# A last MLP whose down projection goes by tokens, in seven block products instead of eight

## The chip, the cores and the metric

The kernel runs on one core of a Trainium2 chip. The metric is the device time of one execution in microseconds. A run of the profiler gives, beside it, every instruction's start and duration on TensorE (PE for products, PEld for loading weights into it), VectorE (DVE), ScalarE (ACT), GpSimd (POOL) and the queue engine SyncE (SP), and the DMA transfers.

## The reference, cut to what matters

The program is a network of two blocks on one sequence of 512 tokens with 1,024 channels. The first has attention, pooling and a state space mixer, then a mixture of experts. The second has two layers: latent attention and an MLP, then an S5 mixer and an MLP. The change is in the last MLP and the last norm, which both layers of the second block compute like this:

```python
def sq_relu_mlp(h, w1, b1, w2, b2):
    a = jax.nn.relu(h @ w1 + b1)
    return (a * a) @ w2 + b2

    shift, scale, gate = modulation(cs, mod_ffn_w[i], mod_ffn_b[i])
    h = x * (1.0 + scale) + shift
    y = sq_relu_mlp(h, mlp_w1[i], mlp_b1[i], mlp_w2[i], mlp_b2[i])
    x = layer_norm_2(ALPHA * x + (1.0 + gate) * y, ln_ffn_g[i], ln_ffn_b[i])
```

Here w1 is 1,024 x 4,096 and w2 is 4,096 x 1,024, both float32; the norm is over the channels of each token.

## The kernel before

Every stage is a block in which each engine has its own instruction list, and semaphores order them; a stage ends when all engines have reached its end. A float32 matrix is split in two float32r parts, `high` (a copy, ScalarE, line 3797) and `low` (matrix minus high part, VectorE, line 3912), and a product is the sum of three: high x high, low x high, high x low (function `three`, line 3722). One product is 128x128 loaded by 512 columns.

`tail_stage` (line 3601) is called twice, for layer 0 (with S5 parameters and the S5 input beside it) and for layer 1 (`last`). It walks over units `n`. A unit is one load of 1,024 KB of weights into one of four buffers `w_second` (line 3679), its high and low part into one of two buffers `late_parts`, and 2 x 8 x 3 = 48 products. Units 0 to 3 are the mixer's output projection, then come the first norm (`mix_norm`) and two steps, each of 8 up units (w1) and 8 down units (w2). All results have channels on partitions and tokens along the row: weights are loaded into TensorE, activations move. The order is written out by hand:

- TensorE starts unit `n` when its low part is done (line 3736).
- ScalarE may write the high part of unit `n + 2` when the products of unit `n` are done (line 3796), since the two buffers alternate. VectorE then makes the low part.
- SP loads unit `n` when the low part of unit `n - 4` is done (line 3678).
- After an up unit ScalarE takes relu out of the banks (line 3820), VectorE squares (3945), ScalarE and VectorE split the square into `hidden` (3826, 3951). During the first step ScalarE also scales the residual `x` (3810).
- After every second down unit VectorE adds gate times the bank to `x` (3927). In the last step it also prepares sums for the norm (3547, 3556, 3564).

The last norm (`TokenNorm`, line 3484) needs sums over partitions, for which TensorE multiplies by a matrix of ones (3504 to 3518). Then come variance and root on rows of 512 tokens (3531 to 3538), centring and scaling of eight channel tiles (3585, 3598), gain and offset (3891), and since the output has tokens on rows, 32 transposes (3788), copies (3830) and eight stores (3695). Small matrices before the norm's end keep TensorE at work (`fill`, line 158).

GpSimd (line 3698) forms a few vectors at a stage's start and has nothing else to do in these stages. In layer 0 of `tail_stage`, VectorE computes S5 parameters between the units (`beside`) into one buffer `room`, which SP stores part by part (line 4077) and VectorE writes again for the next part (line 4310).

## Time and profile before

| | us |
|---|---|
| median of three runs | 2656.68 |
| the three runs | 2660.67, 2656.08, 2656.68 |
| span of the profiled execution | 2654.8 |
| busy TensorE products / weight loads | 2503.1 / 1989.2 |
| busy VectorE / ScalarE / GpSimd | 1729.9 / 1139.0 / 63.4 |
| last MLP stage, first product to end of span | 2221.1 to 2654.8 |
| of it units 4 to 35 | 2281.4 to 2632.2 |

The span is the time from the first to the last instruction of one profiled execution. That execution's time with what lies around the span isn't given apart; the median of the runs is 1.9 us above the span. Busy times of different engines overlap. DMA over the whole: 427.44 MB.

### The profile page before, as it was taken

How to read it: one execution, taken by the hardware profiler on the slowest of the kernel's cores; microseconds unless marked ns; L12 is line 12 of the kernel's file. 1: busy time of each engine (PE TensorE's matmuls, PEld its weight loads, DVE VectorE, ACT ScalarE, POOL GpSimd, SP SyncE). 2: the span in 40 equal slices, each digit the busy share in tenths (PEclk: the TensorE clock that was granted, in tenths of full speed). 3: DMA queues.
4: the chain of work that ended last, by engine and by line, in shares of the span. 5: the costliest groups of instructions: out<-in, count | busy, mean ns of one | idle time of the engine just before them, and what ended most of it. 6: DMA issues, size and time to landing. Idle time of an engine off the chain costs nothing. (4 is left out here: it accounts for less than half of the span.)

```text
span 2654.8 us, 33834 instructions
## 1 busy us (share of the span) xinstructions
PE 2503.1 (94%) x13321; PEld 1989.2 (75%) x13321; DVE 1729.9 (65%) x2508; ACT 1139.0 (43%) x1641; POOL 63.4 (2%) x166
## 2 busy tenths in 40 slices
PE   7999899999989999899988899999999989999998
PEld 5666578777767877788875457888888877788886
DVE  4899545588875666899965565677766664632435
ACT  5444422255564235688853344522324253531323
POOL 0000000000000001000001000000000000000000
PEclk9999999999999988999999999999999899999999
DMA  7887727333235734999962203234332423233321
GB/s 263 264 284 270 245 82 276 91 104 95 80 104 191 257 61 167 355 420 419 417 250 92 78 27 104 80 119 135 111 111 77 127 87 121 65 107 98 95 80 32
DMA packets 299502, 427.44 MB, mean 161 GB/s; under 512 B 27690, under 2 KB 213533, under 8 KB 289488
## 3 DMA queue, kind: packets, MB, share of 16 engines
q1 hardware_dynamic: 289424, 395.13, 43.4%
q0 software_dynamic: 5392, 20.97, 2.0%
q10 hardware_dynamic: 4528, 9.18, 0.9%
q8 instruction: 106, 1.74, 0.3%
q14 instruction: 52, 0.43, 0.0%
HBM read 384.11 MB, written 41.14 MB: 160 GB/s over the span
## 5 line engine op out<-in xcount | busy, mean ns | idle before, releaser
L3724 PE MATMUL banks<-big,late_parts 128*128 128x512 f32 x1920 | 443.0, 393 | 5.9 <-PEq L151 3.8
L3724 PEld LDWEIGHTS banks<-big,late_parts 128*128 128x128 f32 x1920 | 363.3, 189 | 84.1 <-issue 6.1
L3724 PE MATMUL banks<-h_parts_second,late_parts 128*128 128x512 f32 x1440 | 331.1, 390 | 4.7 <-DVE h_parts_second L3936 4.7
L3724 PEld LDWEIGHTS banks<-h_parts_second,late_parts 128*128 128x128 f32 x1440 | 271.0, 188 | 61.2 <-issue 5.1
L3912 DVE TENSOR_TENSOR late_parts<-w_second,late_parts 128x2048 fp32r<-128x2048 f32 x69 | 158.1, 2292 | 218.7 <-ACT late_parts L3797 218.5
L2379 DVE TENSOR_TENSOR expert_parts<-w,expert_parts 128x2048 fp32r<-128x2048 f32 x102 | 232.7, 2288 | 21.7 <-ACT expert_parts L2375 20.8
L3797 ACT ACTIVATE late_parts<-w_second 128x2048 fp32r<-128x2048 f32 x69 | 132.0, 1914 | 255.9 <-PE banks L3724 255.9
L1344 PE MATMUL banks<-h_parts,ssm_parts 128*128 128x512 f32 x960 | 229.0, 396 | 0.8 <-DVE ssm_parts L1611 0.4
L2375 ACT ACTIVATE expert_parts<-w 128x2048 fp32r<-128x2048 f32 x102 | 194.8, 1916 | 60.6 <-PE banks L2386 54.7
L1344 PEld LDWEIGHTS banks<-h_parts,ssm_parts 128*128 128x128 f32 x960 | 178.5, 188 | 43.3 <-issue 6.4
L2386 PE MATMUL banks<-expert_parts,expert_xt 128*128 128x512 f32 x816 | 192.4, 395 | 4.0 <-DVE expert_xt L2367 4.0
L2386 PEld LDWEIGHTS banks<-expert_parts,expert_xt 128*128 128x128 f32 x816 | 153.6, 190 | 36.5 <-DVE expert_xt L2367 4.6
L881 PE MATMUL banks<-h_parts,front_parts 128*128 128x512 f32 x552 | 137.6, 399 | 0.0
L551 PE MATMUL banks<-h_parts,front_parts 128*128 128x512 f32 x576 | 132.3, 391 | 2.7 <-PEq L151 2.7
L551 PEld LDWEIGHTS banks<-h_parts,front_parts 128*128 128x128 f32 x576 | 108.0, 188 | 26.4 <-issue 4.2
L3820 ACT ACTIVATE tail_r<-banks,cols 128x512 f32<-128x512 f32 x64 | 40.5, 685 | 198.5 <-PE banks L3724 198.5
L551 PE MATMUL banks<-h_parts,ssm_parts 128*128 128x512 f32 x480 | 111.5, 394 | 5.9 <-DVE h_parts L1965 3.1
L881 PEld LDWEIGHTS banks<-h_parts,front_parts 128*128 128x128 f32 x552 | 101.5, 190 | 19.7
L3945 DVE TENSOR_TENSOR tail_q<-tail_r 128x512 f32<-128x512 f32 x64 | 41.4, 689 | 111.5 <-ACT tail_r L3820 111.4
L1134 DVE SCALAR_TENSOR_TENSOR attention_mod_sum<-w,silu_c,attention_mod_sum 128x512 f32<-128x512 f32 x147 | 110.4, 751 | 4.8 <-DMA w<-in_mod_ffn_w_dram 0.3
L551 PEld LDWEIGHTS banks<-h_parts,ssm_parts 128*128 128x128 f32 x480 | 91.0, 190 | 26.1 <-issue 3.9
L2386 PE MATMUL banks<-expert_parts,expert_ht 128*128 128x512 f32 x408 | 98.9, 399 | 3.0 <-ACT experts_y L2879 3.0
(703 smaller groups left out, 3851.2 us busy)
## 6 DMA issues: line engine op xcount, KB each, us to landing
w_second<-in_mlp_w_dram SPq DMA_DIRECT2D x64, 1024.0 KB, 5.2
w<-in_w_exp_gate_dram SPq DMA_DIRECT2D x34, 1024.0 KB, 9.6
w<-in_w_exp_up_dram SPq DMA_DIRECT2D x34, 1024.0 KB, 9.4
w<-in_w_exp_down_dram SPq DMA_DIRECT2D x34, 1024.0 KB, 9.2
w<-in_w_in_dram SPq DMA_DIRECT2D x64, 512.0 KB, 4.6
w<-in_mod_mix_w_dram SPq DMA_DIRECT2D x24, 1024.0 KB, 5.1
w<-in_mod_ffn_w_dram SPq DMA_DIRECT2D x23, 1024.0 KB, 5.9
w<-in_w_in_dram SPq DMA_DIRECT2D x16, 1024.0 KB, 5.7
```

The costliest lines, as they stand in the source:

```text
L551: mm = pe.matmul(out, self.parts[:, n % 2, w, kk, f * P:(f + 1) * P], x[:, v, kk, :], start=(start and kk == 0 and j == 0), stop=(stop and ...
L881: mm = pe.matmul(ps[:, bank, :], parts[:, j, w, kk, :], k.hp[:, x, kk, :], start=(kk == 0 and n == 0), stop=(kk == KD - 1 and n == 2))
L1134: ins = dve.scalar_tensor_tensor(out=acc, in0=w, scalar=by, in1=acc, op0=ALU.mult, op1=ALU.add)
L1344: mm = pe.matmul(ps[:, t % 2, :], parts[:, t % SPLITS, w, kk, :], k.hp[:, x, kk, :], start=(kk == 0 and j == 0), stop=(kk == KD - 1 and j ...
L2375: act.activation(self.high_part(h), self.raw(h), ACT.Copy).then_inc(self.high_done, 1)
L2379: dve.tensor_tensor(self.low_part(h), self.raw(h), self.high_part(h).bitcast(F32), ALU.subtract).then_inc(self.low_done, 1)
L2386: mm = pe.matmul(out, x[:, v, first + kk, :], self.tile(h, w, kk), start=(start and kk == 0 and j == 0), stop=(stop and kk == KE - 1 and j ...
L3724: mm = pe.matmul(ps[:, bank(n, f), :], w_part(n, w)[:, kk, f * P:(f + 1) * P], x[:, v, kk, :], start=(first_chunk(n) and kk == 0 and j == ...
L3797: act.activation(w_part(n, 0), raw_half(k, n), ACT.Copy).then_inc(s["high_done"], 1)
L3820: act.activation(r[:, c % 2, :], ps[:, bank(n, c % HT), :], ACT.Relu, bias=k.cols[:, b1 + at:b1 + at + 1]).then_inc(s["relu_done"], 1)
L3912: dve.tensor_tensor(w_part(n, 1), raw_half(k, n), w_part(n, 0).bitcast(F32), ALU.subtract).then_inc(s["low_done"], 1)
L3945: dve.tensor_tensor(q[:, c % 2, :], r[:, c % 2, :], r[:, c % 2, :], ALU.mult).then_inc(s["squared"], 1)
```

## The change

The stage for the last layer becomes a function of its own, `closing_stage`; `tail_stage` keeps layer 0 alone, with one addition, `later.form(pool)`.

- **Seven products.** Each step of the down projection takes a quarter of the hidden channels (1,024). The hidden matrix is seen as 2 x 2 blocks (even and odd tiles of 128 channels by the two halves of the tokens), and the weights as 2 x 2 blocks (even and odd tiles of rows by the two halves of the output channels). Of these, VectorE forms four sums of hidden blocks, and there are seven block products of 24 products each instead of eight; the outputs are sums of these products (the scheme of Strassen and Winograd). Hidden blocks are loaded into TensorE and weights move, so results have tokens on partitions.
- **Four steps** of 4 up units and 7 down units instead of two of 8 and 8: 48 units instead of 36. One up unit of the next step stands ahead of each block of down units, except the last block.
- **Sums of weight blocks.** Four of the seven products need sums of weight blocks. They are formed in DRAM by GpSimd's DMAs during layer 0's MLP: eight transfers of 4 MB, four of which add to their destination.
- **Sums of products.** Two of the seven products (FOUR, 21) stay in their banks over all steps, the other five are added to tiles on chip (`add`) after each unit, and joined in the last step (`join`, `take`).
- **Residual.** `x` is turned to tokens on partitions by 32 transposes after the up units (1,1), (1,2), (1,3) and (2,0), through banks 4 and 5, and copied back by ScalarE.
- **Last norm per token.** GpSimd multiplies sums by the gate (read as a row through DRAM) and adds `x`; VectorE takes mean and variance of each token's row; two token tiles are normed by ScalarE and GpSimd, two by VectorE; four stores of 512 KB.

The core of the diff:

```diff
+class WeightSums:
...
+    def form(self, pool):
...
+        pool.dma_start(two, self.block(0, 0)).then_inc(s["sum_two"], 16)
+        pool.dma_start(right, self.block(0, 1)).then_inc(s["sum_right"], 16)
+        pool.wait_ge(s["sum_two"], 16)
+        pool.dma_start(two, self.block(0, 1), accum_op=ALU.add).then_inc(s["sum_two"], 16)
+        pool.wait_ge(s["sum_right"], 16)
+        pool.dma_start(right, self.block(1, 1), accum_op=ALU.add).then_inc(s["sum_right"], 16)
+        pool.wait_ge(s["sum_two"], 32)
+        pool.dma_start(three, two).then_inc(s["sum_three"], 16)
+        pool.wait_ge(s["sum_three"], 16)
+        pool.dma_start(three, self.block(1, 1), accum_op=ALU.add).then_inc(s["sum_three"], 16)
+        pool.wait_ge(s["sum_three"], 32)
+        pool.dma_start(four, three).then_inc(s["sum_four"], 16)
+        pool.wait_ge(s["sum_four"], 16)
+        pool.dma_start(four, self.block(1, 0), accum_op=ALU.add).then_inc(s["sum_four"], 16)
+        pool.wait_ge(s["sum_right"], 32)
+        pool.wait_ge(s["sum_four"], 32)
...
+PRODUCT_11, PRODUCT_THREE, PRODUCT_RIGHT, PRODUCT_FOUR, PRODUCT_TWO, PRODUCT_22, PRODUCT_21 = range(7)
...
+def closing_stage(k, layer, w_mix, x_parts, big, divided, sums, out):
...
+    BANK = {PRODUCT_11: 4, PRODUCT_THREE: 6, PRODUCT_RIGHT: 4, PRODUCT_FOUR: 2, PRODUCT_TWO: 6, PRODUCT_22: 4, PRODUCT_21: 0}
...
+            sp.dma_start(k.gate_row.rearrange("o (c p) -> p (o c)", p=P), k.mod[:, gate_ffn:gate_ffn + KD], allow_slow_non_contiguous=True).then_inc(s["gate_stored"], 16)
+            for n in range(4, N):
+                if n == N - 2:
+                    sp.wait_ge(s["gate_stored"], 16)
+                    sp.wait_ge(s["tile_done"], tiles_to(N - DOWN - 1))
+                    sp.dma_start(gate, k.gate_row.to_broadcast([P, D])).then_inc(s["gate_loaded"], 16)
+                    for dst, src in ((gain, k.ins["ln_ffn_g_2"][layer:layer + 1]), (shift, k.ins["ln_ffn_b_2"][layer:layer + 1])):
+                        sp.dma_start(dst, src.to_broadcast([P, D])).then_inc(s["rows_loaded"], 16)
+                sp.wait_ge(s["low_done"], n - 3)
+                sp.dma_start(raw(n), source(n)).then_inc(k.raw_loaded[n % 4], 16)
...
+            for first, half, after in ((2, 0, 2), (2, 1, 4), (0, 0, 8), (0, 1, 8)):
+                pool.wait_ge(s["joined"], after)
+                pool.wait_ge(s["w_joined"], 2)
+                for t in (first, first + 1):
+                    pool.tensor_tensor(z(t, half), z(t, half), gate[:, half * STRIP:(half + 1) * STRIP], ALU.mult).then_inc(s["v_step"], 1)
+                    n += 1
+                for j, t in enumerate((first, first + 1)):
+                    pool.wait_ge(s["v_step"], n - 1 + j)
+                    row = z(t, half).rearrange("p (c n) -> p c n", n=P)
+                    pool.tensor_tensor(row, row, x_tile(t, half), ALU.add).then_inc(s["v_ready"], 1)
...
+            def room(i, q, j):
+                if q == PRODUCT_11:
+                    if i > 0:
+                        pe.wait_ge(s["z_step"], reads(i - 1, PRODUCT_22, j))
+                    if i == 1:
+                        pe.wait_ge(s["x_copied"], 2 * TB)
...
+                    for kt in range(4):
+                        pe.wait_ge(s["hidden_low"], UP * i + kt + 1)
+                        for j in range(2):
+                            mm = down_three(n, i, q, j, kt)
...
+            def combine(g):
+                dve.wait_ge(s["relu_done"], HT * (g + 1))
...
+                dve.tensor_tensor(flat, r[:], r[:], ALU.mult).then_inc(s["squared"], 1)
+                dve.wait_ge(s["squared"], g + 1)
+                n = comb.start(dve.tensor_tensor(e[:, LEFT], e[:, FIRST], e[:, SECOND], ALU.subtract))
+                comb.start(dve.tensor_tensor(e[:, SIDE], e[:, BEFORE], e[:, FIRST], ALU.subtract))
+                comb.after(n)
+                comb(dve.tensor_tensor(e[:, ALL], e[:, LEFT], e[:, BEFORE], ALU.subtract))
+                dve.tensor_tensor(e[:, ACROSS], e[:, ALL], e[:, BEHIND], ALU.add).then_inc(s["combined"], 1)
...
+            def take(n, p):
...
+                for j in range(2):
+                    dve.wait_ge(s["tile_done"], HT * n + j + 1)
+                    end(dve.tensor_tensor(tmp(p, j), ps[:, BANK[p] + j, :], gate[:, half * STRIP:(half + 1) * STRIP], ALU.mult))
+                    for first, ready in places:
+                        t = first + j
+                        dve.wait_ge(s["v_ready"], ready + j)
+                        end(dve.tensor_tensor(z(t, half), z(t, half), tmp(p, j), ALU.add))
+                        if (p, first) != (PRODUCT_TWO, 2):
+                            end.start(dve.bn_stats(stats[:, t, half, :], z(t, half)))
...
+            for n in range(RES, N):
+                if up(n):
+                    i, m = up(n)
+                    combine(UP * i + m)
+                    if EXTRA + 1 < n + 2 < N:
+                        low(n + 2)
+                    if i == 0 or m > 0:
+                        hidden_low(UP * i + m)
+                else:
+                    i, p = down(n)
+                    if p in (PRODUCT_11, PRODUCT_THREE, PRODUCT_RIGHT) or (i < STEPS - 1 and p not in KEPT):
+                        add(n)
+                        if i == STEPS - 1:
+                            join(p)
+                    elif i == STEPS - 1:
+                        dve.wait_ge(s["gate_loaded"], 16)
+                        take(n, p)
+                    if n + 2 < N:
+                        low(n + 2)
...
-    tail_stage(k, 1, k.ins["ssm_w_out_2"][0], low_half, big, parts, out=out)
+    closing_stage(k, 1, k.ins["ssm_w_out_2"][0], low_half, big, parts, sums, out)
```

## Rows read from the trace of the kernel before

**Rows 1.** The page: busy time and share of the engines; weight loads and us to landing.

```profile
PE 2503.1 (94%) x13321; PEld 1989.2 (75%) x13321; DVE 1729.9 (65%) x2508; ACT 1139.0 (43%) x1641; POOL 63.4 (2%) x166
...
w_second<-in_mlp_w_dram SPq DMA_DIRECT2D x64, 1024.0 KB, 5.2
```

**Rows 2.** Chain of waits, last MLP: start us, us, what.

```profile
2281.43 306.34 PE banks L3724 x1344
...
2588.62 43.57 PE banks L3724 x192
```

**Rows 3.** Windows: length, busy by engine, clock, DMA; then S5 input products in time order.

```profile
2281.40:2632.20 350.80, 350.77 (x1539) 290.12 (x1540) 140.16 (x142) 111.07 (x122) 0.00 (x0) 1.00 0.24 78
2632.20:2654.80 22.60, 14.94 (x80) 9.75 (x79) 11.82 (x19) 12.45 (x20) 0.00 (x0) 0.89 0.31 93
...
2045.52 22.95 PE L4761 MATMUL banks<-big,h_parts_second 128*128 128x512 f32 x96
```

**Rows 4.** Last 10 us in order of time (start, length), and the stores' landing.

```profile
2648.07 0.42 PEld L3788 LDWEIGHTS banks<-ident,x 128*128 128x128 f32 x4 [0.77 <-ACT x L3891]
2648.07 0.66 PE L3788 MATMUL banks<-ident,x 128*128 128x128 f32 x4 [0.53 <-ACT x L3891]
...
out_dram<-big_plain SPq DMA_DIRECT2D x8, 256.0 KB, 2.2
```

**Rows 5.** In order of time: first products after the first norm, first hand-overs.

```profile
2281.43 2.90 PE L3724 MATMUL banks<-h_parts_second,late_parts 128*128 128x512 f32 x6 [2.37 <-DVE h_parts_second L3936]
...
2303.56 1.27 ACT L3820 ACTIVATE tail_r<-banks,cols 128x512 f32<-128x512 f32 x2 [11.51 <-PE banks L3724]
...
2307.56 1.24 ACT L3820 ACTIVATE tail_r<-banks,cols 128x512 f32<-128x512 f32 x2
...
2308.71 1.90 ACT L3797 ACTIVATE late_parts<-w_second 128x2048 fp32r<-128x2048 f32 x1
...
2310.64 2.29 DVE L3912 TENSOR_TENSOR late_parts<-w_second,late_parts 128x2048 fp32r<-128x2048 f32 x1 [1.09 <-ACT late_parts L3797]
```

**Rows 6.** Groups of instructions: busy us, mean ns of one | idle before.

```profile
L3912 DVE TENSOR_TENSOR late_parts<-w_second,late_parts 128x2048 fp32r<-128x2048 f32 x69 | 158.1, 2292 | 218.7 <-ACT late_parts L3797 218.5
L3797 ACT ACTIVATE late_parts<-w_second 128x2048 fp32r<-128x2048 f32 x69 | 132.0, 1914 | 255.9 <-PE banks L3724 255.9
L3945 DVE TENSOR_TENSOR tail_q<-tail_r 128x512 f32<-128x512 f32 x64 | 41.4, 689 | 111.5 <-ACT tail_r L3820 111.4
...
L4312 DVE TENSOR_TENSOR s_room<-s_room,s_tmp 128x256 f32<-128x256 f32 x32 | 13.6, 425 | 1.1
```

**Rows 7.** Lines 1330, 2719, 2721: ns min/median/max.

```profile
L1330 POOL TENSOR_TENSOR ssm_sq<-ssm_sq x12: 1279/1292/2607, 593.2 to 815.5; 128x512 f32<-128x512 f32 x12
...
L2719 DVE TENSOR_TENSOR routing_room<-expert_parts_plain,routing_both_b x3: 1207/1210/1216, 1055.0 to 1061.1; 128x1024 f32<-128x1024 f32 x3
...
L2721 DVE TENSOR_TENSOR expert_parts_plain<-routing_room,routing_both_b x3: 1925/1934/1991, 1056.3 to 1062.4; 128x1024 f32<-128x1024 f32 x3
```

**Rows 8.** GpSimd and S5 buffer in order of time, then transfers: KB, us to landing.

```profile
1765.74 0.37 SPq L4077 DMA_DIRECT2D s_inputs<-s_room  x1
...
1772.31 0.41 DVE L4310 TENSOR_TENSOR s_room<-s_held,s_b 128x256 f32<-128x256 f32 x1
...
2043.01 1.81 POOL L4249 MEMSET late_parts_plain<- 128x2048 f32 x1 [444.71 <-POOLq L151]
...
expert_rows<-pool_zeros POOLq DMA_DIRECT2D x1, 12288.0 KB, 43.8
...
s_inputs<-s_room SPq DMA_DIRECT2D x8, 512.0 KB, 2.7
```

**Rows 9.** Last MLP's start: first product, then windows (the clock stands third from last).

```profile
2221.12 19.09 PE L3724 MATMUL banks<-big,late_parts 128*128 128x512 f32 x72 [3.76 <-PEq L151]
...
2223.00:2225.00 2.00, 2.00 (x6) 1.61 (x5) 0.68 (x1) 2.00 (x3) 0.10 (x1) 0.50 0.87 231
2225.00:2227.00 2.00, 2.00 (x7) 1.53 (x7) 1.62 (x1) 2.00 (x3) 0.00 (x0) 0.64 0.83 292
```

563 lines of the change are left out of this document (460 added, 103 removed).

## The prediction

> **What bounds the kernel now.** I read the page's busy shares and slices first, then the chain of waits, then the closing stage by windows and in order of time. The page's first lines: TensorE is busy 94% of the span, VectorE 65%, ScalarE 43%, GpSimd 2% [rows 1]. In the stretch that the change rewrites the chain is TensorE alone: 306.34 us without a break, a pair of small sums, and 43.57 us for 192 products [rows 2], that is 226.9 ns per 128x512 product. Its granted clock there is 1.00, VectorE is busy 140 of 351 us, ScalarE 111, the DMA engines 24% [rows 3]. After the last product come 22.6 us (2632.2 to 2654.8) in which the sums over tokens, the norm, eight groups of turns and eight stores hand over to each other, VectorE and ScalarE about 12 us each [rows 3]. So the change can gain in two places, in the number of products and in that end, and it loses wherever a hand-over that had 10.9 us of cover (48 products) now has 5.45 us (24).
>
> **Products.** Before, the last down projection is 16 units of 48 products, 768. Afterwards it is 4 steps of 7 block products, each 2 token tiles x 4 hidden tiles x 3 parts = 24: 672. They have the same form (128x128 loaded, 512 columns moving). 96 x 0.2269 = -21.8 us. The pair of sum products in the middle (0.86) goes too: -0.9. Bounds: below, the same 226.9; above, the S5 input products, 96 in 22.95 us, 239 ns each [rows 3]. These load strided weights, which the new ones don't, so I take 226.9; at 239 the 672 would cost 8 us more.
>
> **Turns.** 32 transposes leave the end and go between up units. Four take 0.42 us of weight loading, 0.66 from the first start to the last end [rows 4]. I take 0.11 each and 0.1 per pair of groups: +3.8 us, bounds 3.4 and 5.3.
>
> **Hand-overs in the up units.** One up unit asks of ScalarE two relus (0.68 each), the high part of a weight tile (1.92), and the high part of seven sums of 256 (1792 columns, by 1.92 for 2048: 1.68); of VectorE a square of 1024 (1.21), four additions of 256 (0.42 each, one overlapped), the weight tile's low part (2.29) and 1792 columns of low part (2.02) [rows 5 to 7]. From the second relu (0.75 after the unit's end) combining ends at 3.6, the next low part at 5.9. That fits under 10.9 us, with three exceptions.
> - First pair. Before, the relus of unit 4 start at 2303.56, those of unit 5 at 2307.56, and unit 7's low part ends at 2312.93, 2.6 us ahead of need (unit 5 ends at 2304.6, unit 6 10.9 later) [rows 5]. Now combining takes 2.8 instead of two overlapped squares (1.3), and the second relu waits behind the longer high part and two residuals: second relu ends at 2312.1, combining at 2315.0, low part at 2317.3: +1.8 us.
> - Up to down. A down unit covers only 5.45 us of the 5.9: +0.45 each time, twice (the third is hidden by the next point).
> - The last turned tiles lie in banks 4 and 5, which the next down product writes. Their copies stand on ScalarE behind relu and a high part: 0.75 + 1.92 + two copies of 0.6 = 3.9 us after the unit, the turns take 0.9: +3.0 us.
>
> **Last change from up to down.** No up unit covers it. The fourth hidden pair needs relu 0.75, combining to 3.6, high part to 5.3, VectorE's weight tile to 5.9 ahead of it, its own low part to 8.0. TensorE has 18 products (4.1 us) of cover: +4.0 us.
>
> **Down units in steady state.** Tile done, high part to 1.95, low part to 4.25, and 5.45 are needed; the additions of product sums (two of 0.68) fit before. Loads: 1,024 KB land in 5.2 us [rows 1]. A load is issued when the low part four units before is done and its high part starts two units before its use, so at 5.45 per unit it has 17 us. I cost the 12 extra loads, 12 high and 12 low parts at nothing: the products hide them with 1.2 us to spare per unit, and what comes on top of that is lost unit by unit. SP also gets a store of 1,024 single values ahead of its first load; that load has 26 us until its high part starts.
>
> **Last step, where VectorE becomes the bound.** Clock from the end of the last up unit (0). With the 4.0 wait, product 11 ends at 9.45, THREE at 14.9, RIGHT at 20.35. After RIGHT VectorE adds (0.7), joins four tiles (2.8) and ends the low part at 26.2, when TensorE wanted it at 25.8: +0.45. After FOUR it multiplies, adds and takes statistics for two tiles; with 0.7 per operation, and GpSimd (1.29 per operation on 512 columns [rows 7]) delivering its first sum at 23.9 + 3 x 1.29 = 27.8, it ends at 31.1, low part 33.4: +1.75. After TWO, six operations and the small aggregations more: low part at 41.7, +2.85. Together 5.05 us, products end at 47.2. Then VectorE still has product 22 (to 45.9), product 21 (to 50.5), four passes of 1024 columns (1.21 [rows 7] and a wait each) to 55.6, and a 512 KB store: 256 KB land in 2.2 [rows 4], 512 KB in 2.7 [rows 8], with its issue 3.1: 58.7. The end shrinks from 22.6 to 11.5: -11.1. No row shows the statistics instruction. A 512-column operation takes 0.69; 256 columns take 0.43 [rows 6] and 1024 take 1.21 [rows 7]; eight of them stand in this chain, so -2 to +4 us around 0.7.
>
> **Clock.** After 3.76 us of idle the granted clock read 0.50 (1.2 GHz) for the next 4 us and 0.64 for two more [rows 9], some 2.7 us lost; after 2.37 us of idle six products took 2.90 [rows 5], where six at 226.9 take 1.36. The waits of 3.0, 4.0 and 2.85 are of this kind. All lost: 8; none: 0; I take +4, since part of the last is hidden behind VectorE.
>
> **The sums of weight blocks** are formed in the MLP before: GpSimd issues eight transfers of 4,096 KB, DRAM to DRAM, four of them adding, six in a row of dependence. GpSimd is idle for 444.7 us there, until 2043.0 [rows 8]. The stage can't end before the last wait there. Its only large transfer now, 12,288 KB, took 43.8 us [rows 8]: 14.6 us for 4,096. Eight at that price, all one after another: 117 us. No row shows an adding transfer; it may cost up to (444.7 - 4 x 14.6) / 4 = 97 us each before it counts. The Trainium skill (Collectives: The Full Stack, "The bandwidth ceiling") says a reducing transfer runs at half the rate of a copy because it reads two sources; by that, as an estimate, 29 us each and 175 us in all, and no run here shows it yet. Beside weight loads, which come 39 us before need and land in 5.2, doubling costs nothing. The tightest user is the S5 buffer: its store lands in 2.7 us, and VectorE writes the buffer again 6.6 us after the issue [rows 8]. I take 0; bounds 0 and rival B.
>
> **Sum.** -21.8 - 0.9 + 3.8 + 1.8 + 0.9 + 3.0 + 4.0 + 5.05 - 11.1 + 4 = -11.25. The profiled execution's span is 2654.8, its own whole time isn't given apart; the median of the three runs, 2656.68, is 1.9 above the span, and I carry that over: **2645.4 us**.
>
> **Rivals.**
> - B, the adding transfers don't fit (slower). For: a transfer that reads, adds and writes 2 KB rows in strict turn has 128 rows per engine (2,048 over 16), and at the 2.2 us of the shortest landing [rows 4] per row it takes 282 us, four take 1,126, 740 us too long: about 3385 us. Against: nothing asks for strict turn, and plain transfers don't behave so. It decides from 97 us per adding transfer; at 100 the gain is gone. Chance 0.09.
> - C, GpSimd is late in the last step. It has sixteen operations there, and all of them read on-chip memory beside VectorE. Its operation took 2.61 once in twelve against 1.29, and a VectorE addition beside its row scatter took 1.93 where the same shape takes 1.21 [rows 7]. At 2.6 each the queue is 16 operations from 12.2: its last four sums come at 40.8, 43.4, 51.2 and 53.8 instead of 27.8 to 34.3; VectorE's low part for 21 moves from 41.7 to 57.6, +15.9: 2661 us, no gain. Chance 0.08. The Trainium skill (SBUF — State Buffer, "Who interferes with whom") states that a VectorE instruction with two inputs there contends with a GpSimd one that reads; by that rule this is what would happen, while by the median of the rows it isn't.
> - D, the hand-overs cost more than I sum, half clock after each wait (+4) and statistics at 1.2 (+4), and the turns at their bound (+1.5): 2655, no measurable change. Chance 0.11.
> - E, the middle waits vanish, since copies and residuals find gaps: the 3.0, 1.8 and the clock's 4 go: 2637. Chance 0.10.
> - Forecast: 0.62.
>
> **Range and chances.** About 0.2% (5.3 us) can be told from no change. Of the forecast's 0.62 nearly all is faster; with E and a little of C and D: faster 0.73. Same: most of D, half of C: 0.14. Slower: B and the rest: 0.13. B is left out of the range, its far end can't be held: 2635 to 2659.
>
> **What would show it.** 672 down and 768 up products at 227 ns each. TensorE idle: one wait near 4 us ahead of the last block, one near 3 us behind the last turns, two or three in the last 30 us that end on VectorE's low part. Less than 12 us from the last product to the end. GpSimd's last wait of the stage before well ahead of 2043, and that stage as long as now. It is wrong if that stage grows, if down units before the last step wait for weights, or if the end is longer than 16 us.

## The result: slower by 0.9%, where 0.4% faster was forecast

| | median us | runs | ratio to before, 95% interval |
|---|---|---|---|
| before | 2658.39 | 2656.08 to 2660.67 (4) | |
| changed | 2682.34 | 2679.82 to 2689.42 (4) | 1.0093 (1.0076 to 1.0109) |
| forecast | 2645.4 | range 2635 to 2659 | |

The profiled execution of the changed kernel took 2689.42 us, its span is 2687.7 (before: 2654.8). It is the slowest of its four, so I compare stages and not whole spans; each stage is read from one profiled execution. Stages are cut at GpSimd's operations, which stand at the start of each: the MLP of layer 0 from the first operation on `vec` to the fill of `late_parts`; the S5 and GLU stages from there to the next operation on `vec`; the last MLP from there to the end.

| us | MLP of layer 0 | S5 and GLU | last MLP |
|---|---|---|---|
| before | 450.3 | 178.1 | 433.7 |
| changed | 474.0 | 184.2 | 434.0 |
| forecast of the difference | 0 | 0 | -11.25 |
| measured | +23.7 | +6.1 | +0.3 |

So two things went wrong: a loss in a stage that I had costed at nothing, and a gain that didn't come in the stage that was rewritten. The medians of the whole lie 23.95 us apart, which is what the two MLPs give together (23.7 + 0.3).

The +0.3 flatters the change. After the same wait of 3.76 us at the start of the last MLP, the first 96 products took 24.53 us in the kernel before (granted clock 0.73 over the first 10 us) and 23.42 in the changed one (0.85); after the same wait of 2.37 us behind the first norm, the first twelve took 4.25 and 2.84 (0.67 and 1.00 over 4.6 us). No edit touches these; both kinds of start occur among the profiles of kernels that share this code. Start for start, the changed stage is 2.8 us longer. A difference of under 3 us between two last MLPs can be of this kind.

The page of the changed kernel, the lines that answer to [rows 1] (the engine's busy us and share; the weight loads of both MLPs and us to landing):

```profile
PE 2489.4 (93%) x13175; PEld 1975.2 (73%) x13175; DVE 1821.9 (68%) x2578; ACT 1166.0 (43%) x1632; POOL 118.8 (4%) x196
...
w_second<-in_mlp_w_dram SPq DMA_DIRECT2D x60, 1024.0 KB, 5.3
```

TensorE is busy 13.7 us less (2503.1 to 2489.4). Fewer products alone should give 21.8; part of the difference is that products last longer at a lower granted clock (the last three blocks below take 5.9 us more than three times 5.45). VectorE is busy 92 us more. The median landing of a weight tile hides what happened. In the MLP of layer 0, from 1590 to 1700 us, the tiles land so (least, median, most us):

```profile
DMA to landing us min/median/max: 18.0/43.2/54.1
```

ScalarE's operations on them in order of time (start, length; in brackets idle before and what ended it):

```profile
1650.24 1.91 ACT L3828 ACTIVATE late_parts<-w_second 128x2048 fp32r<-128x2048 f32 x1 [13.17 <-DMA w_second<-in_mlp_w_dram]
1663.87 1.91 ACT L3828 ACTIVATE big<-w_second 128x2048 fp32r<-128x2048 f32 x1 [11.72 <-DMA w_second<-in_mlp_w_dram]
```

and TensorE's waits for the norm behind them:

```profile
1658.69 2.07 PE L3510 MATMUL banks<-tail_sums,ones 128*128 128x512 f32 x2 [11.30 <-DVE tail_sums L3557]
1667.87 2.07 PE L3512 MATMUL banks<-tail_sums,ones 128*128 128x512 f32 x2 [7.11 <-DVE tail_sums L3565]
```

In the kernel before the same stretch has 5.2/5.3/8.8 us to landing. This is a chain: the tile is late, ScalarE is stuck on its high part with the squares of the norm queued behind it, VectorE's sums are late, TensorE is idle. ScalarE's two waits make 24.9 us. TensorE waits 19.9 us for the norm's sums (11.30, 7.11 and one more of 1.51), where the kernel before has one wait of 1.29; the stage's other 5 us go with a granted clock of 0.87 instead of 0.98 from 1593 to 1700 us.

In the last MLP TensorE's waits (in brackets), in order of time from the first hand-over:

```profile
2346.53 22.06 PE L4191 MATMUL banks<-h_parts_second,late_parts 128*128 128x512 f32 x96 [0.74 <-DVE late_parts L4394]
2374.42 32.93 PE L4209 MATMUL banks<-late_parts,big 128*128 128x512 f32 x144 [0.40 <-DVE late_parts L4394]
2457.45 39.97 PE L4209 MATMUL banks<-late_parts,big 128*128 128x512 f32 x168 [2.97 <-ACT x L4322]
2546.78 32.94 PE L4209 MATMUL banks<-late_parts,big 128*128 128x512 f32 x144 [0.39 <-DVE late_parts L4394]
2620.13 14.92 PE L4209 MATMUL banks<-late_parts,big 128*128 128x512 f32 x54 [3.69 <-DVE big L4421]
2635.62 5.73 PE L4209 MATMUL banks<-late_parts,big 128*128 128x512 f32 x24 [0.57 <-DVE late_parts L4394]
2644.77 7.39 PE L4209 MATMUL banks<-late_parts,big 128*128 128x512 f32 x24 [3.42 <-DVE late_parts L4394]
2656.38 7.14 PE L4209 MATMUL banks<-late_parts,big 128*128 128x512 f32 x24 [4.22 <-DVE late_parts L4394]
2668.86 7.69 PE L4209 MATMUL banks<-late_parts,big 128*128 128x512 f32 x24 [5.34 <-DVE late_parts L4394]
```

Down to 2620 these are the waits that the prediction named, at its prices or below. Then come 13.6 us in four waits where it had 5.05 in three. Behind the last three of them, a block of 24 products takes 7.1 to 7.7 us instead of 5.45: over its first 4 us the granted clock reads 0.50 to 0.75. In the kernel before it was 1.00 up to the last product and 0.89 over the end behind it [rows 3]; from the last step to the end it is now 0.81:

```profile
2612.20:2687.70 75.50, 47.10 (x169) 36.34 (x167) 63.45 (x60) 19.24 (x22) 42.40 (x20) 0.81 0.21 77
```

(columns as in [rows 3]: VectorE busy 63.45 of 75.50, GpSimd 42.40). From VectorE's operations of that step, in order of time:

```profile
2623.82 1.29 DVE L4440 TENSOR_TENSOR closing_sums<-closing_sums,closing_z_late 128x512 f32<-128x512 f32 x2
2630.36 3.00 DVE L4445 TENSOR_TENSOR closing_z_late<-closing_z_late,closing_sums 128x512 f32<-128x512 f32 x2
2633.28 2.28 DVE L4394 TENSOR_TENSOR late_parts<-w_second,late_parts 128x2048 fp32r<-128x2048 f32 x1
2635.49 1.27 DVE L4432 TENSOR_TENSOR big_plain<-big_plain,banks 128x512 f32<-128x512 f32 x2
2636.79 3.42 DVE L4448 TENSOR_TENSOR big_plain<-big_plain,closing_sums 128x512 f32<-128x512 f32 x2
2648.42 1.68 DVE L4467 TENSOR_TENSOR big_plain<-big_plain,closing_r 128x512 f32<-128x512 f32 x1 [3.11 <-POOL big_plain L4179]
2650.13 0.69 DVE L4469 BATCH_NORM_STATS2 closing_stats<-big_plain 128x6 f32<-128x512 f32 x1
2664.50 4.31 DVE L4394 TENSOR_TENSOR late_parts<-w_second,late_parts 128x2048 fp32r<-128x2048 f32 x1
```

and from GpSimd's:

```profile
2625.34 4.52 POOL L4174 TENSOR_TENSOR closing_z_late<-closing_z_late,h_parts_second_plain 128x512 f32<-128x512 f32 x2 [48.86 <-DVE closing_sums L4440]
2633.44 4.53 POOL L4174 TENSOR_TENSOR closing_z_late<-closing_z_late,h_parts_second_plain 128x512 f32<-128x512 f32 x2 [0.63 <-DVE closing_z_late L4445]
2663.99 2.67 POOL L4185 TENSOR_TENSOR big_plain<-big_plain,h_parts_second_plain 128x1024 f32<-128x1024 f32 x1
```

Two additions of 512 columns take 1.29 alone, 3.00 and 3.42 beside GpSimd. A low part takes 2.28 where it began first (2633.28 against 2633.44) and GpSimd's pair beside it takes 4.53 (2.58 by the 1.29 of [rows 7]); it takes 4.31 where GpSimd was first (2663.99 against 2664.50). Additions that read a product's bank (1.27 for two) and the statistics (0.69) keep their length.

### The profile page after: what moved, and what is told of

It is laid out like the page before. It is cut to its first block and busy times, and to the rows that moved or that the text cites. A ratio compares the mean times of both kernels' runs of the same rounds, so it can differ in the third digit from the quotient of the medians.

```text
span 2687.7 us, 33664 instructions
## 1 busy us (share of the span) xinstructions
PE 2489.4 (93%) x13175; PEld 1975.2 (73%) x13175; DVE 1821.9 (68%) x2578; ACT 1166.0 (43%) x1632; POOL 118.8 (4%) x196
## 5 line engine op out<-in xcount | busy, mean ns | idle before, releaser
L3766 PE MATMUL banks<-big,late_parts 128*128 128x512 f32 x960 | 221.0, 392 | 2.2 <-DVE late_parts L3919 2.2
L1345 PEld LDWEIGHTS banks<-h_parts,ssm_parts 128*128 128x128 f32 x960 | 180.5, 190 | 43.6 <-issue 6.5
L3766 PEld LDWEIGHTS banks<-big,late_parts 128*128 128x128 f32 x960 | 181.3, 189 | 41.0 <-DVE late_parts L3919 2.4
L4209 PE MATMUL banks<-late_parts,big 128*128 128x512 f32 x672 | 164.2, 406 | 21.0 <-DVE late_parts L4394 14.3
L4209 PEld LDWEIGHTS banks<-late_parts,big 128*128 128x128 f32 x672 | 132.0, 198 | 52.5 <-DVE late_parts L4394 16.9
L4394 DVE TENSOR_TENSOR late_parts<-w_second,late_parts 128x2048 fp32r<-128x2048 f32 x46 | 107.7, 2340 | 57.0 <-ACT late_parts L4289 56.9
L3919 DVE TENSOR_TENSOR late_parts<-w_second,late_parts 128x2048 fp32r<-128x2048 f32 x35 | 80.1, 2292 | 93.2 <-ACT late_parts L3828 93.1
L4289 ACT ACTIVATE late_parts<-w_second 128x2048 fp32r<-128x2048 f32 x46 | 88.0, 1913 | 118.3 <-PE banks L4209 105.5
L3828 ACT ACTIVATE late_parts<-w_second 128x2048 fp32r<-128x2048 f32 x35 | 66.9, 1914 | 143.3 <-PE banks L3766 130.1
L552 PEld LDWEIGHTS banks<-h_parts,front_parts 128*128 128x128 f32 x576 | 109.2, 190 | 26.8 <-issue 4.2
```

Source lines behind the costliest of these rows:

```text
L552: mm = pe.matmul(out, self.parts[:, n % 2, w, kk, f * P:(f + 1) * P], x[:, v, kk, :], start=(start and kk == 0 and j == 0), stop=(stop and ...
L1345: mm = pe.matmul(ps[:, t % 2, :], parts[:, t % SPLITS, w, kk, :], k.hp[:, x, kk, :], start=(kk == 0 and j == 0), stop=(kk == KD - 1 and j ...
L3766: mm = pe.matmul(ps[:, bank(n, f), :], w_part(n, w)[:, kk, f * P:(f + 1) * P], x[:, v, kk, :], start=(first_chunk(n) and kk == 0 and j == ...
L3919: dve.tensor_tensor(w_part(n, 1), raw_half(k, n), w_part(n, 0).bitcast(F32), ALU.subtract).then_inc(s["low_done"], 1)
L4209: mm = pe.matmul(ps[:, BANK[q] + j, :], hidden(STATIONARY[q], v)[:, kt, j * P:(j + 1) * P], strip_part(n, w)[:, kt, :], start=(kt == 0 and ...
L4289: act.activation(w_part(n, 0), raw_half(k, n), ACT.Copy).then_inc(s["high_done"], 1)
```

## The experiments

Each line gives the stages as above; the last column is the whole time's ratio to the kernel before, run on the same chip, with its interval.

| kernel | MLP of layer 0 | last MLP | median us | ratio |
|---|---|---|---|---|
| b_form | 476.8 | 433.7 | 2681.07 | 1.0086 (1.0070 to 1.0103) |
| e_late | 503.6 | 434.1 | 2713.38 | 1.0215 (1.0198 to 1.0232) |
| e_s5 | 454.3 | 435.1 | 2662.70 | 1.0020 (1.0009 to 1.0031) |
| e_attn | 449.1 | 434.0 | 2701.10 | 1.0158 (1.0139 to 1.0177) |
| e_swap | 470.0 | 433.8 | 2680.30 | 1.0079 (1.0053 to 1.0105) |
| e_split | 450.4 | 437.1 | 2659.46 | 1.0006 (0.9997 to 1.0016) |
| c_nopool | 478.4 | 422.9 | 2679.62 | 1.0081 (1.0058 to 1.0104) |
| c_fix | 474.1 | 429.7 | 2683.60 | 1.0095 (1.0072 to 1.0118) |
| c_scratch | 476.7 | 438.1 | 2694.26 | 1.0137 (1.0112 to 1.0162) |
| c_all | 477.4 | 430.9 | 2686.45 | 1.0109 (1.0083 to 1.0135) |
| g_turns | 474.4 | 429.5 | 2683.82 | 1.0100 (1.0081 to 1.0119) |
| best | 450.5 | 421.0 | 2648.81 | 0.9967 (0.9955 to 0.9980) |

The kernels with the transfers at the old place or in the attention spread by 5 to 12 us between their own runs, so there a whole time tells less than a stage. The last MLP of kernels that don't touch it took 433.7 to 435.1, but for e_split's 437.1. Of its 3.1 us over the changed kernel, 1.5 lie in the first 96 products (24.91) and 1.6 in the twelve behind the first norm (4.42), the slow start told above. The last step by itself, from the end of the last up unit to the end of the span, is the cleaner number: 75.5 us in the changed kernel, e_late, e_attn, e_swap and e_split (74.0 in e_s5).

The diffs below are excerpts. Those of the last MLP's runs are shortened to what they do, and some lines in them are words and not code.

### Where the 24 us in the MLP of layer 0 come from

**b_form**, one part alone:

```diff
 # kernel before, GpSimd in the MLP of layer 0
             step(pool.tensor_scalar(vec[:, O_SHIFT], sh2, ALPHA_2, None, ALU.mult))
+            later.form(pool)
```

> One part of the change alone: the kernel before, and in the MLP of layer 0 GpSimd also issues the eight transfers that form the sums of weight blocks, right after its column work, as in the changed kernel. Nobody reads the sums. Theory T (the transfers delay the first weight tiles of that MLP, the rest of the change is about even): that MLP goes from 450.3 us to about 474, and the whole time from 2658.4 to 2682 (2678 to 2686), the whole loss of the change. Rival R1 (the loss is a difference of placement, alignment or code between the programs): the MLP stays within 3 us of 450.3 and the whole within 5 us of the kernel before.

476.8 in the stage, 2681.07 in all. The transfers, which nobody reads here, cost the kernel before what the whole change cost. Theory T holds.

**e_late** and **e_s5**, the start of the transfers:

```diff
+            pool.wait_ge(s["low_done"], 12)        # e_late
+            pool.wait_ge(s["dt_loaded"], 32)       # e_s5
+            pool.wait_ge(s["b_loaded"], 64)        # e_s5
             later.form(pool)
```

> The changed kernel with one wait more: GpSimd starts the eight transfers only when the twelfth weight tile of the MLP of layer 0 is divided, when the small S5 loads have long landed and loads run ahead of need. Theory T1 (only the first tiles suffer, because there the loads start with nothing in hand): the MLP is back at 450 to 453, the whole at 2657 to 2662, level with the kernel before. Rival T2 (plain share of the bandwidth: 28 MB more have to pass at any time, and the weight tiles lose as much later): the MLP stays at 465 or more, the whole above 2672.

503.6 and 2713.38. Theory T1 failed, and rival T2's bounds came by another mechanism than it named: it was not the weight tiles. The first waits are gone, a worse one is there. The S5 buffer `s_room` from 1750 to 1900 us: for how many us and times VectorE stood idle for its stores, and the stores' landing:

```profile
  DMA s_inputs<-s_room: 70.8, 7
...
DMA to landing us min/median/max: 9.1/10.4/26.7
```

TensorE's first waits behind it:

```profile
1798.63 14.05 PE L3767 MATMUL banks<-big,late_parts 128*128 128x512 f32 x48 [12.03 <-DVE late_parts L3920]
1816.57 13.65 PE L3767 MATMUL banks<-big,late_parts 128*128 128x512 f32 x48 [3.89 <-DVE late_parts L3920]
1839.72 13.98 PE L3767 MATMUL banks<-big,late_parts 128*128 128x512 f32 x48 [9.49 <-DVE late_parts L3920]
```

The stores of 512 KB land in 10.4 us instead of 2.7 [rows 8], VectorE writes the buffer again after 6.6, stands still, and its next low part, which TensorE needs, is late. The prediction had named this buffer as the tightest user, with both numbers, and then taken 0.

> The changed kernel with another wait: GpSimd starts the eight transfers when the six S5 loads that stand ahead of the weight loads in SyncE's queue (8,192 pieces of 64 bytes the largest) have landed, still before the first up products. Theory T1a (in the changed kernel 709 packets of SyncE's queue carried 0.05 MB in 10 us while 765 of GpSimd's carried 3.13 MB: packet by packet in turn, the small pieces are held up behind the large): most of the loss goes, the MLP falls to 450 to 458 and the whole to 2658 to 2667. Rival T1b (the weight tiles are slow at half a share, 14 us per MB while GpSimd's transfers add, whatever stands ahead): 12 us or more stay, the whole above 2671.

454.3. A start 4.7 us later, behind the small loads, gives back 20 of 24 us: ScalarE has no wait for these tiles any more. Of the 4 us that stay, 3.51 are one wait of TensorE behind VectorE, which stood 14.8 us for the S5 buffer's stores. How the two queues share, in the changed kernel from 1606 to 1616 us, and from 1636 to 1646, while two transfers add (packets, MB, share of the 16 engines; q0 carries GpSimd's transfers, q1 SyncE's):

```profile
q0 software_dynamic: 765, 3.13, 95.5%
q1 hardware_dynamic: 707, 0.05, 4.9%
```

```profile
q0 software_dynamic: 748, 1.53, 82.4%
q1 hardware_dynamic: 742, 0.75, 27.8%
```

Packet for packet the queues get nearly the same number; small packets carry 0.05 MB in the time in which large ones carry 3.13. The Trainium skill (DMA: Bandwidth & Descriptors, "Queues, rings and completion order") says that a DMA engine takes turns between queues packet by packet; the trace agrees: 765 packets against 707, and in e_swap below, from 1630 to 1680 us, 4,419 against 4,416 (11.12 MB and 0.79). The prediction did not weigh it.

**e_swap** tells the order from the share of the bandwidth:

```diff
-            beside.load(sp, s)
             for n in range(4, N):
                 ...
+                if n == 6:
+                    beside.load(sp, s)
```

> The changed kernel with its transfers where they were, and the order in SyncE's queue turned round: the six small S5 loads are issued behind the first three weight tiles of the MLP of layer 0 instead of ahead of them (in the kernel before the values of the first are used near 1682 us). Theory T1a (the weight tiles were late because 8,192 small pieces ahead of them in their queue went one for one with GpSimd's large packets): the first weight tile lands 12 to 20 us after its issue instead of 47, ScalarE's waits for it (13.2 and 11.7) go, the MLP takes 452 to 460 and the whole 2659 to 2668; what remains is the S5 loads' own lateness and the second place, the buffer's stores. Rival T1b (half a share of the bandwidth, whatever stands ahead): the tile still lands after more than 30 us, ScalarE waits 10 us or more, the MLP stays above 468.

The first waits went as T1a says: ScalarE starts the two tiles at 1636.55 and 1638.35 without waiting (1650.24 and 1663.87 in the changed kernel). But the stage fell only to 470.0 and the whole to 2680.30, where at most 460 and 2668 were expected, a miss of 10 and 12 us. The hold-up moved behind the small loads. SyncE's queue in order of time (start and length of the issues):

```profile
1621.99 29.41 SPq L4589 DMA_DIRECT2D s_room<-in_ssm_b_re_dram  x2
1651.44 44.22 SPq L4589 DMA_DIRECT2D s_room<-in_ssm_b_im_dram  x2
1695.70 16.70 SPq L3727 DMA_DIRECT2D w_second<-in_mlp_w_dram  x4
```

and TensorE's wait for the first of those tiles:

```profile
1708.04 24.56 PE L3767 MATMUL banks<-h_parts_second,late_parts 128*128 128x512 f32 x96 [15.09 <-DVE late_parts L3920]
```

The issue of four small loads, 1.9 and 2.7 us for two each in the kernel before, took 73.6: SyncE could not go on, and the next tiles were issued only at 1695.70. Whatever stands behind the small pieces waits; which tile that is depends on the order. Large transfers beside the tiles alone are not the cause: in e_s5 the tiles land in 24.8 us at the median there (35.9 at most), also far from 5.3, and TensorE waits for them no more than 0.56 us.

**e_attn**, another stage for the transfers:

```diff
 # attention of the second block
+        @block.gpsimd
+        def _(pool):
+            later.form(pool)
 # MLP of layer 0
-            later.form(pool)
+            later.ready(pool)       # the last two waits of form
```

> The changed kernel with the eight transfers moved one stage ahead: GpSimd issues them in the attention of the second block, where the kernel before has its DMA engines busy 13 to 24% from 1400 to 1590 us and GpSimd idle for 165 us; only the wait for the last two stays in the MLP of layer 0. Theory T (the transfers cost time only where somebody needs a transfer soon: the small S5 loads with the first weight tiles behind them, and later the S5 buffer's stores): the MLP is at 450 to 452 again, the attention longer by 0 to 4 us (its loads of 192 and 128 KB are issued most of a head ahead), the whole at 2657 to 2662. Rival T3 (any 28 MB of adding transfers disturb whatever runs beside them, by the memory and not by the queue): the attention is longer by 10 us or more, or the MLP stays above 460, and the whole is above 2668.

The MLP is at 449.1, but the whole at 2701.10. The attention waits for its own loads, which land in 9.0 and 11.6 us instead of 2.5 and 2.6, and the stage's end waits until the last transfer has landed: issued at 1609.18, landed 25.1 us later at 1634.3. From TensorE in order of time:

```profile
1470.46 3.68 PE L3298 MATMUL banks<-cq,latent_attention_wq 128*64 128x512 f32 x4 [7.07 <-DMA latent_attention_wkv<-in_mla_w_kvb_dram]
1503.77 3.63 PE L3298 MATMUL banks<-cq,latent_attention_wq 128*64 128x512 f32 x4 [10.37 <-DMA latent_attention_wkv<-in_mla_w_kvb_dram]
1634.98 5.91 PE L158 MATMUL banks<-ident 128*128 128x128 f32 x28 [23.10 <-PEq L151]
```

DMA engines 13 to 24% busy were no room: these loads are small and each is needed within a head. Theory T's number for the attention (0 to 4 us) was wrong, and the rival's (10 or more) came, but by waits that can be named; 23.1 us of it are the end of the stage.

**e_split** uses what the four showed:

```diff
+            pool.wait_ge(s["dt_loaded"], 32)
+            pool.wait_ge(s["b_loaded"], 64)
             later.form(pool)
 # in form, ahead of "four"
         pool.wait_ge(s["sum_three"], 32)
+        pool.wait_ge(s["low_done"], 27)
         pool.dma_start(four, three).then_inc(s["sum_four"], 16)
```

> The changed kernel with the eight transfers placed by what needs the queues: the first six after the S5 loads have landed (as in e_s5), the last two (copy to four, add to four) only when the 27th weight tile of the MLP is divided, behind the stage's eight stores of the S5 buffer that follow each other unit by unit. In e_s5 what was left of the loss were two waits of TensorE of 0.56 and 3.51 us, the second behind VectorE, which had waited 14.8 us in three times for the S5 buffer's stores. Theory T4 (both users named): the MLP takes 450 to 452 us, TensorE has no wait of 2 us or more for low parts in it, the whole is 2656 to 2662, level with the kernel before. Rival T5 (adding transfers slow the MLP at any place by their bandwidth): the MLP stays at 454 or more, the whole at 2662 to 2670.

450.4, as before, and TensorE has no wait in the stage that the kernel before hasn't. The S5 buffer's stores land in a median of 2.8 us. 1.0006 (0.9997 to 1.0016): once both users are out of their way, no cost of the transfers can be told in the stage, and none beyond about 4 us in the whole, which also holds the last MLP's own loss. T4 holds.

### Where the gain in the last MLP went

**c_nopool**, **c_fix**, **c_scratch** on the last step:

```diff
-    z = z * gate; z = z + x            # GpSimd, 16 operations
-    dve.wait_ge(s["v_ready"], ready + j)
     # c_nopool: no more than that (VectorE unchanged)
     # c_fix: VectorE does it all, in place of tmp = product * gate; z = z + tmp
+    z = z + product;  z = z * gate;  z = z + x
     # c_scratch: c_fix, and GpSimd on a tile of its own, at the old points
+    scratch = scratch * gate;  scratch = scratch + x
```

> The changed kernel; left out of the computation are GpSimd's sixteen operations in the last step (gate times sum, plus x) and VectorE's waits for them, so the gate and x parts of the output are missing. VectorE's program is otherwise as it was. Theory C (in the last step GpSimd's and VectorE's operations with two inputs in on-chip memory slow each other down: the inflation of VectorE's operations sums to 13.5 us, its wait for GpSimd to 3.1): VectorE's operations there fall to their clean durations (additions of 512 columns 0.69, low parts 2.29), the closing stage from 434.0 to 418 to 422 and the whole from 2682 to 2667 to 2670. Rival C2 (VectorE's long operations come from its own pieces, statistics and small waits, or from memory banks of the last tiles): durations stay, only the 3.1 goes, the closing stage stays above 429.

> The changed kernel with GpSimd's sixteen operations of the last step given to VectorE: VectorE adds the product to the sum, multiplies by the gate and adds x in place, 28 operations with one statistics each instead of 20; GpSimd keeps the four passes of the norm. The output is complete. Theory C (the two engines slow each other down there, leaving GpSimd out gave 11.1 us in the closing stage): eight more operations at 0.72 cost 5.8 of the 11.1, the closing stage takes 428 to 430 against 434.0, the whole 2674 to 2680. Rival C3 (VectorE is the bound of the last step by its own work, and any operation moved to it costs its full time with nothing back): the closing stage takes 437 to 440, the whole 2685 to 2688.

> The same program of VectorE as in c_fix (the output is complete); beside it GpSimd does two fills and its sixteen operations of before on a tile of its own that nobody reads, begun at the same points, and VectorE doesn't wait for it. Theory C (contention lengthens VectorE's operations with two inputs in on-chip memory, whoever needs the result): those operations and the low parts show 1.2 to 4.3 us where c_fix has 0.69 and 2.29, the closing stage takes 8 to 14 us more than c_fix. Rival C4 (what cost time was the wait for GpSimd's results and the order it forced, not durations): within 2 us of c_fix.

422.9 without GpSimd's operations (11.1 less; its output lacks the gate and x parts), 429.7 with VectorE doing them, 438.1 when GpSimd does work that nobody waits for beside it. The last step alone takes 65.0, 71.1 and 79.6 us against 75.5. The pair c_fix and c_scratch has the same program on VectorE; the 8.4 us between their stages, 8.5 between their last steps, are the contention alone. c_nopool's stage lies 0.9 above its range. The medians of the whole of c_nopool and c_fix (2679.62, 2683.60) lie above my ranges, by more than the MLP of layer 0 explains (478.4 and 474.1): c_fix's is not below the changed kernel's 2682.34. The profiled spans, 2677.4 and 2679.6, are nearer. What these runs show is the stage and its durations; no gain in the whole is shown by them. Groups of VectorE operations from 2610 to 2690 us (busy us, mean ns), first c_fix:

```profile
L4457 DVE TENSOR_TENSOR big_plain<-big_plain,x 128x512 f32<-128x512 f32 x4 | 2.8, 693 | 0.1
L4454 DVE TENSOR_TENSOR big_plain<-big_plain,h_parts_second_plain 128x512 f32<-128x512 f32 x4 | 2.8, 692 | 0.1
L4451 DVE TENSOR_TENSOR big_plain<-big_plain,banks 128x512 f32<-128x512 f32 x4 | 2.7, 678 | 0.0
```

and the same three in c_scratch:

```profile
L4474 DVE TENSOR_TENSOR big_plain<-big_plain,x 128x512 f32<-128x512 f32 x4 | 4.7, 1174 | 0.1
L4471 DVE TENSOR_TENSOR big_plain<-big_plain,h_parts_second_plain 128x512 f32<-128x512 f32 x4 | 5.1, 1264 | 0.1
L4468 DVE TENSOR_TENSOR big_plain<-big_plain,banks 128x512 f32<-128x512 f32 x4 | 2.7, 676 | 0.0
```

693 becomes 1174 with two inputs in on-chip memory; with one of them in a product's bank it stays at 676. The rule that the prediction set beside rival C (the Trainium skill, SBUF — State Buffer, "Who interferes with whom") is borne out, and so is its exception for one input, as far as that input's partner lies in a product's bank.

**c_all** gives the norm of the first two tiles to VectorE as well, and moves the next low part ahead of each product's work:

```diff
+    low(n + 2)
     take(n, p)
-    low(n + 2)
+    if p == PRODUCT_22: last_norm(0); last_norm(1)
```

> As c_fix, and the norm's last passes of the first two token tiles by VectorE too (GpSimd does nothing in the last step), and in the last step VectorE forms the low part of the next weight tile ahead of the work on the product just done. Theory C: in the run without GpSimd's sixteen operations its two passes of 2.4 and 4.4 still lengthened four VectorE operations by 6.1 us in all (a low part took 4.31 instead of 2.29); four passes of 1.28 on VectorE cost 5.1; and TensorE waits less for low parts in the last step (waits together below 3 us against 13.6), which gives nothing by itself as VectorE is the bound: the closing stage takes 426 to 430, the whole 2672 to 2679. Rival C5 (VectorE has no room for 5.1 more, and the norm's two tiles by GpSimd are nearly free): 3 us or more above c_fix.

430.9, just above the stated range and 1.2 above c_fix, so no gain is shown. The whole, 2686.45, lies 7 us above its range. GpSimd's norm had lengthened four operations in c_fix by about 5.6 us; four passes of 1.28 cost 5.1; and in its new place VectorE waited 1.90 for ScalarE's high part. TensorE's waits for weight tiles fell to below 1 us together and gave nothing: VectorE is the bound.

**g_turns**, the other hand-overs:

```diff
-    turned tiles after the up units (1,1) (1,2) (1,3) (2,0)
+    turned tiles after the up units (1,1) (1,2) (1,3) (2,1)
 # VectorE behind the last up unit
-    low(n + 2); hidden_low(...)
+    hidden_low(...); low(n + 2)
```

> The changed kernel with two hand-overs of its last MLP moved: the fourth pair of turned tiles is made after the second up unit of the third step (not right ahead of the second down step), and after the last up unit VectorE forms the low part of the hidden pair ahead of the weight tile's. The transfers stay as they were. My terms for the two waits were 3.0 and 4.0 (measured 2.97 and 3.69). If the terms are what I took them for, the first falls to 0.4 or less with nothing new before the third down step, the second to 1.4 with at most 0.6 new ahead of the next block product, the granted clock dips less, and the closing stage takes 428.5 to 431 against 434.0; the whole follows by 3 to 5 us (2677 to 2680). Rival: behind each wait stood another (the hidden pair's low part; VectorE and GpSimd as the bound of the last step, who would then begin earlier but end no earlier): less than 2 us in the stage.

429.5, 4.5 less, of which 4.1 lie ahead of the last step and 0.4 in it (75.1). The whole, 2683.82, is above its range and not below the changed kernel. The wait of 2.97 is 0.39 now. The second fell only from 3.69 to 3.34: behind VectorE's order stood ScalarE's high part of the hidden pair (in best, with the same order, VectorE is idle 1.76 for it). So the size of the first was right and of the second the cause was wrong.

**best** puts it together: e_split, g_turns, and the last step by VectorE with each operation over two tiles.

```diff
+    a = pair(first, half)                                  # two token tiles, 1,024 columns
+    a = a + ps[:, BANK[p]:BANK[p] + 2, :];  a = a * gate;  a = a + x
     # low parts behind take as in the changed kernel; last_norm(0), last_norm(1) behind product 22
```

> All that the runs point to together: transfers as in e_split, hand-overs as in g_turns, the last step's operations by VectorE alone (GpSimd idle), each over two token tiles at once (1,024 columns: 1.25 instead of two of 0.72), the norm of all four tiles by VectorE with the first two ahead of the last block product. Closing stage: c_fix's 429.7, less 3.7 and 1 to 1.5 for the hand-overs, less 2 to 3 for the paired operations, less 0.5 for the norm: 421 to 425 against 433.7 of the kernel before; the MLP 450 to 452; the whole 2645 to 2652. Rival (gains overlap, since VectorE is the bound of the last step): closing stage 426 to 429, the whole 2652 to 2656, hardly to be told from the kernel before.

421.0 in the stage (66.5 in the last step), 450.5 in the MLP, 2648.81 in all, 0.9967 (0.9955 to 0.9980): faster than the kernel before by a third of a percent, all inside the expected ranges. Start for start, the last MLP is some 10 us shorter than before and not 12.7; the medians of the whole differ by 8.35. TensorE's waits in its last step:

```profile
2585.32 25.27 PE L4193 MATMUL banks<-late_parts,big 128*128 128x512 f32 x102 [3.34 <-DVE big L4402]
2612.24 5.74 PE L4193 MATMUL banks<-late_parts,big 128*128 128x512 f32 x24 [1.65 <-DVE late_parts L4375]
2620.81 5.78 PE L4193 MATMUL banks<-late_parts,big 128*128 128x512 f32 x24 [2.83 <-DVE late_parts L4375]
```

## Why the prediction was wrong

Two steps failed. Of the first the prediction named the place (the S5 buffer) and not the waits that came; the second stood in it as rival C.

- **The sums of weight blocks, "I take 0; bounds 0 and rival B".** This is the 24 us (b_form). The argument compared averages: a tile lands in 5.2 us and is issued 39 ahead of need, so twice 5.2 is harmless. The first tile of this stage is issued behind the small loads, 34 us ahead of need (1602.88; ScalarE stood free for it from 1637.07), and landed after 47.3 us; the slowest of the stretch took 54.1, ten times 5.3 and not twice. In place of the 0 the changed kernel shows 23.7, and b_form 26.5 for the same transfers; only where they are placed as in e_split is it 0.1. The bound from above asked only when the transfers must be finished (97 us each); they were done by about 1780 of 2069. Rival B, that they don't fit, was the wrong worry: they fitted and still took a queue's turns. The size of one transfer was about right. The last adding transfer took 30.1 us beside weight loads and the copy ahead of it 15.6; in e_attn the last adding transfer, with all engines idle, took 25.1 and the copy ahead of it 16.1. By the Trainium skill (Collectives: The Full Stack, "The bandwidth ceiling") the prediction had estimated 29, a copy's price doubled; the traces have factors of 1.9 and 1.6. Where two ran at once it was up to 53.8.
- **"Last step, where VectorE becomes the bound."** That VectorE bounds it was right; its and GpSimd's durations were taken as if each ran alone. From the end of the last up unit (2620.13 - 3.69 - 4.1 = 2612.3) to the end it took 75.4 us against 58.7: 16.7 more, of which the clock's +4, booked apart, was forecast. Rival C had this place, this mechanism and +15.9, and got 0.08, because the median row of [rows 7] was clean. That row shows GpSimd's side alone. The trace of the kernel before has the other side; the same VectorE addition of 384 columns, first without GpSimd, then 0.16 us behind the start of its operation at 669.19:

```profile
667.65 0.56 DVE L1715 TENSOR_TENSOR x<-x,ssm_xbc 128x384 f32<-128x384 f32 x1
669.35 1.55 DVE L1715 TENSOR_TENSOR x<-x,ssm_xbc 128x384 f32<-128x384 f32 x1
```

Three of GpSimd's eleven clean operations have such an addition beside them, at 1.55 each time; the one of 2.61 began at 808.14, behind a low part of VectorE that had begun at 807.31 and kept its 2.29. So who began second paid, and the contention was there to be read before the change. In the last step nearly every operation of either engine has two inputs in on-chip memory. Of the 16.7, c_nopool shows 10.5 (75.5 to 65.0 in this step); some of the rest is the norm's passes by GpSimd, still there in that run (a low part of 4.31), and the clock.

The other terms: the turns 0.8 for each group of eight, 3.2 in all (3.8 forecast); first hand-over 0.74 (1.8); up to down 0.40 and 0.39 (0.45 each); the turned tiles 2.97 (3.0); the last up to down 3.69 (4.0); from the last product to the end 11.1 (11.5: last block starts at 2668.86, ends 7.69 later, span 2687.7). With GpSimd's sixteen operations left out, which is what the forecast took them to cost, the stage is 10.8 under the kernel before (9.3 start for start), where -11.25 was forecast. So the other terms together hold to about 2 us.

Left open: the S5 and GLU stages, 178.1 before and 184.2 after. Over all profiles they took 178.1 to 184.2 without an order that fits any edit (b_form 178.6, c_nopool 179.0, best 180.1, e_split 184.1), so I hold the 6.1 for no part of the change. Also open is why TensorE's clock after the same wait comes back sooner in some executions than in others.

## What to carry to other kernels

A background transfer isn't priced by its bandwidth or by when it must be done, but by who has a short transfer in flight beside it: look up, for its whole time, each small load and each buffer written again soon after its store, and start or stop it around them. Work given to GpSimd beside a VectorE that is the bound is not off the path when both read two operands from on-chip memory; let VectorE do it over wider tiles. When a rival names the mechanism of the place, price it by how often the condition holds there, not by a median from elsewhere, and read both engines' durations before calling a row clean.

## What the runs showed of the hardware that I had not expected

- The issue of a load is held up itself beside such traffic: 73.6 us for SyncE's four issues of small loads in e_swap, 4.5 in the kernel before (1.85 and 2.69 for two each). A weight tile's issue behind the small loads took up to 21.0 in the changed kernel, 1.5 at most before.
- A stage's end waits for GpSimd's transfer in flight although nobody waited for it in that stage: 23.10 us of idle TensorE in e_attn, from 1611.9 to 1635.0; the last adding transfer was issued at 1609.18 and landed at 1634.3.
- A VectorE addition that reads a product's bank keeps 0.68 us beside a busy GpSimd where one with both inputs in on-chip memory goes from 0.69 to 1.2 on average and 2.75 at most (c_fix, c_scratch). One input on chip is not safe in every form: in the kernel before, three TENSOR_SCALAR operations of 512 columns that began 0.4 us behind a GpSimd operation took 1.12, where others of that line take 0.54.
- After the same wait of 3.76 us the same 96 products took 23.4 to 23.6 us in some profiles and 24.5 to 24.9 in others, with the granted clock of the first 10 us at 0.83 to 0.85 and 0.69 to 0.74.
- An operation of VectorE over 1,024 columns took 1.22 where two over 512 take 1.38 and a gap.
